# A hybrid decoder layer with expert retrieval: the places of the ranked picks made on ScalarE, the pick taken as a maximum on VectorE, and the gathered rows between GpSimd's scatter groups counted in eights

## What is computed

```python
q = (xn @ w_query).reshape(T, 8, 2, 128)
s = einsum('thpc,hpkc->thpk', q, sub_keys)              # 8 heads, 2 halves, 128 keys each
s1, i1 = top_k(s[:, :, 0], 16); s2, i2 = top_k(s[:, :, 1], 16)
cand_s = (s1[..., :, None] + s2[..., None, :]).reshape(T, 8, 256)
cand_i = (i1[..., :, None] * 128 + i2[..., None, :]).reshape(T, 8, 256)
top_s, pos = top_k(cand_s, 16)
idx = take_along_axis(cand_i, pos); gates = softmax(top_s)   # 128 experts per token
...
out[t] = sum_k gates[t,k] * gelu(expert_u[idx[t,k]] . x[t]) * expert_v[idx[t,k]]
```

## Time and profile before

| | |
|---|---|
| median of 3 runs | 2668.53 us (2666.84 to 2668.69) |
| profiled execution | 2672.46 us, of which the span is 2670.7 us |
| TensorE, VectorE, ScalarE, GpSimd busy | 2516.4, 2021.1, 347.0, 1439.3 us |

### The profile page before, as it was taken

How to read it: one execution, slowest core, us unless ns; L and a number is a source line. 1 busy time by engine, 2 the same in 40 slices (tenths; PEclk the granted TensorE clock), 3 DMA queues, 4 the chain that set the end, 5 groups by cost and what they waited for, 6 DMA issues and landing times.

```text
span 2670.7 us, 24061 instructions
## 1 busy us (share of the span) xinstructions
PE 2516.4 (94%) x7657; PEld 1384.2 (52%) x7657; DVE 2021.1 (76%) x4251; ACT 347.0 (13%) x657; POOL 1439.3 (54%) x1168
## 2 busy tenths in 40 slices
PE   7999999998688999999999999999999999999992
PEld 5687786866566444444444444444444444444441
DVE  2207877689588499888887967769788687887988
ACT  1112112111488100000000010000000000001010
POOL 0000120884861167676765767757567686766765
PEclk9999999999799999999999999999999999999996
DMA  6544764665497889989999999999999999999998
GB/s 259 219 153 156 267 223 153 163 169 170 107 264 220 323 333 365 395 309 397 356 401 403 388 413 363 383 395 398 414 396 393 395 364 420 396 414 394 403 399 315
DMA packets 285902, 857.88 MB, mean 321 GB/s; under 512 B 41936, under 2 KB 97232, under 8 KB 271184
## 3 DMA queue, kind: packets, MB, share of 16 engines
q0 software_dynamic: 167040, 541.20, 54.1%
q1 hardware_dynamic: 108464, 289.97, 28.9%
q10 hardware_dynamic: 10272, 25.17, 2.4%
HBM read 807.94 MB, written 48.30 MB: 321 GB/s over the span
## 4 chain that ended last, share of the span: by engine, by line
PE 21%; DMA 15%; POOL 11%; issue 7%; DVE 5%; DVEq 0%; another core or an unknown queue 0%; ACT 0%; POOLq 0%; ACTq 0%
PE pairs L711 13%; DMA ring<-in_expert_u,idx 11%; POOL ring L570 11%; PE pairs L669 8%; DMA ring<-in_expert_v,idx 4%; DVE junk L1018 2%; DVE arena L1029 1%; DVE scratch L972 0%; DVE half_i L974 0%; DVE scratch L969 0%; DVEq L971 0%; DVE dots L1018 0%; DVE arena L1085 0%; DVE xf L1029 0%
## 5 line engine op out<-in xcount | busy, mean ns | idle before, releaser
L570 POOL DMA_INDIRECT ring<-in_expert_u,idx x512 | 657.0, 1283 | 632.1 <-DVE dots L1018 355.9
L711 PE MATMUL pairs<-arena 128*128 128x512 f32 x2048 | 891.1, 597 | 14.7 <-DVE arena L1079 14.0
L669 PE MATMUL pairs<-arena 128*128 128x512 f32 x2048 | 884.5, 593 | 3.0 <-ACT arena L836 3.0
L1018 DVE CUSTOM_DVE_ANT_0 junk<-ring,xf 128x1024 bf16<-128x1024 f32 x512 | 611.8, 1223 | 211.7 <-DMA ring<-in_expert_u,idx 205.1
L570 POOL DMA_INDIRECT ring<-in_expert_v,idx x512 | 564.8, 1103 | 291.4 <-issue 131.3
L711 PEld LDWEIGHTS pairs<-arena 128*128 128x128 f32 x2048 | 391.3, 191 | 512.1 <-issue 510.8
L669 PEld LDWEIGHTS pairs<-arena 128*128 128x128 f32 x2048 | 389.1, 190 | 490.9 <-issue 490.9
L1029 DVE SCALAR_TENSOR_TENSOR arena<-ring,arena 128x1024 f32<-128x1024 f32 x381 | 472.2, 1282 | 99.6 <-DMA ring<-in_expert_v,idx 98.7
L590 PE MATMUL pairs<-arena 128*128 128x272 f32 (+1 forms) x2048 | 462.6, 388 | 13.3 <-DVE arena L1103 7.3
L590 PEld LDWEIGHTS pairs<-arena 128*128 128x128 f32 x2048 | 391.4, 191 | 83.4 <-DVE arena L1103 7.7
L545 POOL DMA_INDIRECT gate_tables<-gate,place x128 | 211.4, 1651 | 149.8 <-DVE gate L1037 109.1
(11 more groups left out here) (143 smaller groups left out, 1047.0 us busy)
## 6 DMA issues: line engine op xcount, KB each, us to landing
arena<-in_w_all SPq DMA_DIRECT2D x80, 1024.0 KB
arena<-in_uT SPq DMA_DIRECT2D x128, 512.0 KB
arena<-in_expert_v SPq DMA_DIRECT2D x128, 512.0 KB
arena<-gate_tables SPq DMA_DIRECT2D x32, 1024.0 KB
gate_tables<-arena SPq DMA_DIRECT2D x12, 2048.0 KB
gate_tables<-junk ACTq DMA_DIRECT2D x4, 2048.0 KB, 13.5
ring<-in_expert_u,idx POOLq DMA_INDIRECT x512
ring<-in_expert_v,idx POOLq DMA_INDIRECT x512
```

Source lines behind the costliest of these rows:

```text
L570: nc.gpsimd.indirect_dma_start(out=ring[:, r % RING, :], out_offset=None, in_=expert_u if table == "u" else expert_v, in_offset=bass.Indir ...
L669: last = nc.tensor.matmul(score_bank[x], uslot[:, x % USLOTS, k * P:(k + 1) * P], xfT[:, k, :], start=(k == 0), stop=(k == KD - 1))
L711: last = nc.tensor.matmul(o_bank[n % 4], gated[:, x % GSLOTS, t * P:(t + 1) * P], vrows[:, j, half * 512:(half + 1) * 512], start=(j == 0) ...
L1018: nc.vector.tensor_tensor_reduce(out=junk[:, r % 2, :], in0=row, in1=xf[:, t % 2, :], scale=1.0, scalar=0.0, op0=ALU.mult, op1=ALU.add, ac ...
```

## The change

1. **Pick.** Before, VectorE did 12 instructions for a tile (4 units of compare with an iota, multiply with `topi`, reduce by sum, 1024 float32 each). Now ScalarE writes, in 16 activations of 256 elements, `(32*digit - 32*a)^2` in bfloat16 (zero where the digit is `a`, at least 1024 elsewhere; `pick_places`). VectorE subtracts this from the key numbers in bfloat16 (`topf`, cast in `digits`) and reduces by a maximum: two instructions of 4096 elements. ScalarE waits for `digits_ready`, VectorE for `hot_ready`.
2. **Buffers.** `pick_hot`, `cand`, `left` and `g_final` share one buffer, `pick_all`. `g_final` is therefore loaded later, by GpSimd, ahead of the rows of `("u", 2)`.
3. **Planner.** New costs for `digits`, `pick` and `keep`; the second tile's first two `keys` units stand between `digits` and `pick` of the first; a `pick` is not dealt before `PLACES_US` have passed since its `digits`, and rows fill that time.
4. **Scatters and rows.** The planner limits the rows ahead of the batches to a count: 21 before `spread`, then 8, then 16 more in group 3. GpSimd's heads 0 and 1 follow row 28, heads 2 to 4 row 36, heads 5 to 7 row 44. Before, they followed rows 17, 17, 19, 22, 25, 27, 30 and 33.

The planner's numbers that come out: `spread` stands behind row 9 before and behind row 20 now; ahead of the batches VectorE uses 29 rows before and 45 now; ahead of `order` 41 and 57; behind the last `sum` 29 and 28.

```diff
-        COST = {"keys": 6.8, "cands": 1.4, "pairs": 6.2, "digits": 3.4, "pick": 3.9, "keep": 1.5, "spread": 1.5, "row": 1.35}
+        COST = {"keys": 6.8, "cands": 1.4, "pairs": 6.2, "digits": 3.7, "pick": 7.0, "keep": 1.2, "spread": 1.5, "row": 1.35}
+        PLACES_US = 10.0
...
+        def ranking_of_two(r):
+
+            one, two = ranking_of(r), ranking_of(r + 1)
+            return one[:8] + two[:2] + one[8:] + two[2:]
...
+                row_ready = rows < row_limit and (0 if rows < HK else 1) in ranked
+                if to_rank and not (to_rank[0][0] == "pick" and since_digits < PLACES_US):
                     unit = to_rank.pop(0)
...
+                elif unit[0] == "spread":
+                    scatter_from, row_limit = rows, rows + RING
...
+                elif GT * (n - 1) > SCATTER_RANK:
+
+                    two[5:5] = [("row", 0, 0)] * RING
+                    row_limit += 2 * RING
...
-            head_after = [scatter_from + RING - 1 + (scatter_to - scatter_from) * max(0, h - 1) // (HEADS - 1) for h in range(HEADS)]
+            head_after = [scatter_from - 1 + RING * (1 + (h + 1) // 3) for h in range(HEADS)]
...
+                    if t == 2:
+
+                        pool.wait_ge(routed, GATHERED)
+                        pool.dma_start(g_final, rows_g[:, D:2 * D]).then_inc(g_final_in, 16)
...
+            def pick_places(r):
+                act.wait_ge(digits_ready, r + 1)
+                if r == 0:
+                    act.wait_ge(place16_ready, 1)
+                for a in range(TOPK):
+                    last = nc.scalar.activation(pick_hot[:, :, :, :, a].rearrange("p h s k -> p (h s k)"), digit[:].rearrange("p h s k -> p (h s k)"),
+                                                ACT.Square, scale=32.0, bias=place16[:, a:a + 1])
+                last.then_inc(hot_ready, 1)
...
-            def pick(q):
...
+            def pick(r):
+
+                dve.wait_ge(hot_ready, r + 1)
+                flat = pick_hot.rearrange("p h s k a -> p (h s) k a")
+                nc.vector.tensor_tensor(flat, topf[:].rearrange("p h s a -> p (h s) a").unsqueeze(2).to_broadcast([P, HP, TOPK, TOPK]), flat, ALU.subtract)
+                dve.drain()
+                nc.vector.tensor_reduce(half_i[:].rearrange("p s (h k) -> p h s k", h=HEADS), pick_hot, AX.X, ALU.max)
```

More of the change, by code:

```diff
@@ L330, in take, with step_at @@
             return got
-        QUERY_US = 14.2
-        exp_after = None
+        TURN_US, QUERY_US = 17.0, 14.2
+        def step_at(n, where, us):
+            if where == "query":
+                i = int((us - TURN_US) // QUERY_US)
+                return ("query", n, min(i, 3)) if i >= 0 else ("turn", n, GT - 1)
+            return {"conv0": ("bcv", n, 1), "conv1": ("bcv", n, 2), "conv2": ("bcv", n, 3), "conv3": ("bcv", n, 4),
+                    "gate": ("bcv", n, 5), "y": ("ynorm", n, 0), "outp": ("ynorm", n, 0)}[where]
@@ L336, in program @@
+        exp_after, picks_after, scatter_from = None, {}, 0
         for n in range(GRPS):
             if n > 0:
-                one, two = ranking_of(GT * (n - 1)), ranking_of(GT * (n - 1) + 1)
+                two = ranking_of_two(GT * (n - 1))
                 if GT * (n - 1) == SCATTER_RANK:
-                    two.insert(2, ("spread", 0, 0))
-                to_rank += one + two
+                    two.insert(two.index(("keep", SCATTER_RANK, 0)) + 2, ("spread", 0, 0))
+                elif GT * (n - 1) > SCATTER_RANK:
+                    two[5:5] = [("row", 0, 0)] * RING
+                    row_limit += 2 * RING
+                to_rank += two
@@ L342, in program @@
             for where, us in FILL:
                 plan[n, where] = take(us)
[L344 to L350, removed]
+                if (n, where) == (GRPS - 1, "query"):
+                    plan[n, where] += to_rank
+                    to_rank = []
@@ L351, in program @@
+                spent = 0.0
+                for unit in plan[n, where]:
+                    spent += COST[unit[0]]
+                    if unit[0] == "digits":
+                        picks_after.setdefault(step_at(n, where, spent), []).append(unit[1])
+                    elif unit == ("keep", SCATTER_RANK, 0):
+                        exp_after = step_at(n, where, spent)
         assert not to_rank
-        scatter_to = rows
+        row_limit = 2 * HK
         for b in range(BATCHES):
@@ L408, in program @@
                     early.append(ROWS[a // HK][1])
+            elif kind == "digits":
+                beside[x].append(("places", a))
             elif kind == "keep" and a == TILES - 1:
@@ L737, in spread_after, with picked_after @@
                     nc.scalar.activation(gate[:], gate[:], ACT.Exp).then_inc(s_exped, 1)
+            def pick_places(r):
[6 more added lines that the diff above has]
+                last.then_inc(hot_ready, 1)
+            def picked_after(step):
+                for r in picks_after.get(step, ()):
+                    pick_places(r)
             square_x(0)
@@ L856, in _ @@
                 for kind, t in beside[x]:
-                    if kind == "exp":
+                    if kind == "places":
+                        pick_places(t)
+                    elif kind == "exp":
                         act.wait_ge(shifted, GATHERED)
@@ L980, in keep @@
                 if r == SCATTER_RANK:
[L982 to L983 removed]
+                    a, b = work[:, 0:HK], work[:, HK:2 * HK]
+                    ju, jh = (work[:, n * HK:(n + 1) * HK].bitcast(U32) for n in (2, 3))
                     nc.vector.tensor_tensor(gate[:].rearrange("p (h k) -> p h k", h=HEADS), best[:], low, ALU.subtract).then_inc(s_shifted, 1)
@@ L1048, in unit @@
                 elif kind == "pick":
-                    pick(b)
+                    pick(a)
                 elif kind == "keep":
@@ L1089, in unit @@
                     dve.drain()
-                    nc.vector.scalar_tensor_tensor(out=sums[:, a, :], in0=sums[:, a, :], scalar=col[:, 5 + a:6 + a], in1=g_final[:],
+                    nc.vector.scalar_tensor_tensor(out=sums[:, a, :], in0=sums[:, a, :], scalar=col[:, 5 + a:6 + a], in1=g_final,
                                                    op0=ALU.mult, op1=ALU.mult).then_inc(d_out, 1)
```

62 lines of the change are left out of this document (35 added, 27 removed).

## The result

The changed kernel took **2736.86 us** (median of 4 runs, 2734.20 to 2738.82), the kernel before beside it 2667.78 (4 runs): a ratio of 1.0258, interval 1.0241 to 1.0276. It is slower by 2.6%; 0.6% was forecast, and the range ended at 2699. The sign and the one long wait were right, the size was not.

The account below looks back on a forecast made before the run. TensorE was taken to set the dense phase's pace, with row transfers just behind. Batches ending 23.2 us later, less 5.3 (dense) and 1.2 (tail), gave +16.7 us: 2685 us against 2668.53, range 2673 to 2699.

Parts of the forecast that it names:

- The sign: Whole kernel: slower than before, chance 0.84.
- the one long wait: VectorE, behind the fourth batch: one wait of 40 to 50 us for a transfer, ending near 747.
- Pick: Each tile: VectorE saves 5 to 12 us; ScalarE gets 16 activations of 0.496 us, 7.9 us.
- Start of the chain: GpSimd's scatter queue starts at 467.26, as before, when the gates of `spread` are there.
- Rows without a wait in the mixer: End of mixer: VectorE's waits of 21.75 and 28.98 us go; batches start some 20 us earlier, at 688 to 695.
- What is late next: Row 45, behind all 128 scatters, issued at 742.2, usable at 746.6; batches end 23.2 us later.
- Dense phase and tail: Dense products: 5.3 of TensorE's 13.3 us of waits go; behind the last product, one row fewer saves 1.2 us.
- The sum: Whole kernel: +23.2 - 5.3 - 1.2 = +16.7 us, 2685 us; chance 0.70 for 2676 to 2694.
- Slower still: Dearer scatters (2.04 us, shift 36) or a later start of GpSimd's queue: 2704 us; chance 0.14 for above 2694.
- Faster: The mixer's gain goes through, row 45 never holding VectorE: 2642 us; chance 0.06.
- A scatter's price beside a busy VectorE: GpSimd's heads 5 to 7: a scatter takes 1.925 us beside a busy VectorE, 1.855 while VectorE waits.

Follow-up runs that it names:

- flat places: Changed kernel with ScalarE writing each place as 256 elements in a row instead of every sixteenth element: 2707.74 us, ratio 1.0174.
- old pick, new plan: Changed kernel with VectorE picking as before and no places on ScalarE; order, rows and heads kept: ratio 1.0209, mended 1.0201 against the kernel before.
- the cheap one: Changed kernel with heads 6 and 7 later, places and VectorE's keys in a row, and maxima of halves instead of a reduction: 2626.77 us, ratio 0.9877.
- later heads: Changed kernel with only GpSimd's heads 6 and 7 moved, behind rows 47 and 50: 2690.76 us, ratio 1.0106.
- both edits: Changed kernel with places written in a row and heads 6 and 7 behind rows 47 and 50: 2644.64 us, ratio 0.9938; again 2645.21 us, 0.9950.

## Why the prediction was wrong

Times in us: three points of time and, in the last column, a length.

| kernel | first scatter | row 45 issued | dense starts | from there to the end |
|---|---|---|---|---|
| before | 467.3 | | 913.1 | 1757.6 |
| forecast | 467.3 | 742.2 | 936.3 | 1751.1 |
| changed | 504.9 | 788.6 | 984.1 | 1750.7 |
| flat places | 477.5 | 768.5 | 963.0 | 1740.5 |
| old pick, new plan | 486.7 | 775.4 | 970.7 | 1742.5 |

The rule behind the sum holds in the three measured kernels of the new order: row 45 leaves 284 to 291 us after the first scatter, and the dense products begin 194.5 to 195.6 us after row 45. Point by point:

- **Pick: the step that failed.** "ScalarE gets 16 activations of 256 elements, 0.496 us each as L773, 7.9 us a tile." They take 17.75 us. L773 has the same number of elements, but writes them in a row. In a row the places cost 6.5 us. VectorE's two instructions, 2.4 to 9.8 us together, took 6.7: right.
- **Start of the chain: the step that failed with it.** "`spread` still stands one `keys` unit behind `keep`, so I leave this." True of the order, not of the time. It moved by 37.6 us: 27.4 go with the slow places (504.9 against 477.5), and 10.2 stay without them. With the old pick it is 19.4, with the cheap one 5.6 (472.8), each give or take the 5 us between two executions. So it follows what the pick takes. The rest may be the 21 rows instead of 10 that stand ahead of it, which was not tried alone; its cause stays open.
- **Rows without a wait in the mixer.** Right: no wait like those of the earlier trace rows. "The batches start at 688 to 695": with flat places the last wait ahead of them ends at 694, with slow ones at 738.
- **What is late next.** Right in place and kind, 42.84 us for row 45, shown by the run in which later heads take it away. The chain took 283.7 us instead of 274.9: heads 0 and 1 67.8 (65.2), heads 2 to 4 99.8 (95.6), heads 5 to 7 95.9 (93.7), the rows as forecast. That term is 8.8 us short. 5.9 of it are the five waits for a landing, 1.5 to 4.1 us each beyond the usual 0.3 between two scatters, where 1.6 was forecast; the rest are dearer scatters in heads 2 to 7.
- **Dense phase and tail.** Forecast -6.5, measured -7.0, but the agreement is luck. TensorE's waits behind its first run were to fall by 5.3 us and fell by half a microsecond (13.3 to 12.8). Its busy time was to be unchanged, and fell by 5.6, from 1697.1 to 1691.5 us for the same 3928 instructions, at a mean granted clock of 1.00 instead of 0.99. With places in a row, or with the old pick, the whole term is -15 to -17, more than the 14.5 that "more can't" allowed, and the slow places of the last tiles take 8 to 10 back.
- **The sum.** +16.7 was forecast, +64.1 came. Of the 47.4 between, 37.6 are the start, 8.8 the chain, 1 what lies behind.
- **The rivals.** "Slower still" named this very mechanism ("activations that write every sixteenth element may take longer than 0.496 us"), but gave it "some us" and a chance of 0.14; the bounds of the unknown cost were not carried into the range. "Faster" was refused on right grounds. That its 2642 lies near the 2644.64 of both edits is partly chance: it was to be 20 us from the mixer and 6.5 behind, and the first run of both edits has 13.7 ahead of the dense products and 14.9 behind.
- **A scatter's price beside a busy VectorE.** The row behind it, 1.925 us against 1.855, is an average over unlike work. Head 6 begins at 727.46 beside ranking and short instructions of VectorE, head 7 at 758.80 in VectorE's wait, and in both the scatters stand 1.86 us apart. The dear ones lie mostly under VectorE's gathered rows (below). By the Trainium skill's rule for the shared port ("SBUF — State Buffer", section "Who interferes with whom"), as the prediction used it, only casts and scalar operations would hold a scatter, and the sum would be 1.4 us smaller. The same section says that a VectorE instruction with two inputs in SBUF contends with a GpSimd instruction that reads SBUF; a gathered row has the inputs `ring` and `xf`, a scatter reads `gate` and `place`, and here the trace agrees.

## What to carry to other kernels

When work moves to an idle engine, price it by a row that has the same output step and element size, not only the same number of elements, and ask what stands still until it is done. Where one queue holds a chain of fixed length and a transfer behind it, the chain's start is a term of its own, and an improvement ahead of the wait disappears in it: 44 us of the mixer came out as 20 until two heads were moved back by three and six rows. With the place as outermost dimension and those two heads moved, the same change went from 2.6% slower to 0.5% faster.

## What was unexpected of the hardware

- ScalarE writes bf16 at every 16th element at 1.09 us for 256 elements, fp32 at the same distance in bytes at 0.52, either in a row at 0.41. Why narrow elements suffer so much more is open.
- A scatter that GpSimd issues while VectorE uses gathered rows takes longer. In the changed kernel the 11th to the 14th scatter of head 0 stand 2.3 us apart instead of 1.86, while VectorE uses eight rows, one every 1.15 us: two rows go by for each scatter. Timeline, both engines:

```profile
521.67 1.55 POOL L579 DMA_INDIRECT gate_tables<-gate,place  x1 [0.30 <-issue]
...
522.84 1.23 DVE L1073 CUSTOM_DVE_ANT_0 junk<-ring,xf 128x1024 bf16<-128x1024 f32 x1 [0.20 <-issue]
523.53 1.96 POOL L579 DMA_INDIRECT gate_tables<-gate,place  x1 [0.30 <-issue]
...
525.79 1.99 POOL L579 DMA_INDIRECT gate_tables<-gate,place  x1 [0.30 <-issue]
...
530.86 1.22 DVE L1073 CUSTOM_DVE_ANT_0 junk<-ring,xf 128x1024 bf16<-128x1024 f32 x1
...
532.67 1.55 POOL L579 DMA_INDIRECT gate_tables<-gate,place  x1 [0.30 <-issue]
```

  The same stands in the kernel with both edits, 26 us earlier (rows from 496.43, dear scatters from 497.12), and in the kernel before at other numbers of the chain (rows from 505.94, scatters 2.29 us apart from 508.90). Over the changed kernel the ten scatters that lie at least 1.4 us under rows take 2.01 us on average, the 115 that touch none 1.60. Some other instructions of VectorE with two inputs have a dear scatter beside them too, but not each of them. No edit was made to test this.
- A bf16 subtraction of 4096 elements takes 2292 ns where both inputs have 16 elements in a row, and 4425 where one is repeated along the innermost dimension.
